# Block two's activations moved by 64 bytes in the on-chip memory

## The reference, cut to what matters

```python
h  = concat([meta_tokens, x])                 # 16 + 256 tokens
hn = rms_norm(h, norm_mix_g)
u, gb_in, gc_in, v_in, ga_lin, gbr_lin = split(hn @ w_in)
y_a = (pooled(u) @ pool_w per group) * pool_scale     # trailing means over 2, 4, 8, 16 tokens
y_b = (gb_in * conv3(gc_in * v_in)) @ conv_out_w
g_a, g_b = split(sigmoid([ga_lin, gbr_lin] + b_gate))
h   = h + (g_a * y_a + g_b * y_b) @ w_o
hn  = rms_norm(h, norm_ffn_g)
gate, up = split(hn @ w_gate_up)              # 2048 -> 2 x 5632
h   = h + (silu(gate) * up) @ w_down          # 5632 -> 2048
out = rms_norm(h, norm_final_g)[16:]
```

## Time and profile before

| what | us |
|---|---|
| median of 3 runs | 3395.7 |
| the runs | 3390.18, 3395.7, 3415.17 |
| the profiled execution, its own time | 3380.61 |
| its span, first to last instruction | 3379.3 |
| first matmul of block two's projections, from the span's start | 1893.8 |
| last of them | 3366.2 |

### The profile page before, as it was taken

One profiled execution on the slowest core, in us unless ns is written; L12 is line 12 of the kernel. 1 busy time (PEld: TensorE's weight loads), 2 busy tenths in 40 slices (PEclk: granted clock), 3 DMA queues, 4 the chain that ended last, 5 costly groups with the idle time before them and its releaser, 6 DMA issues.

```text
span 3379.3 us, 52152 instructions
## 1 busy us (share of the span) xinstructions
PE 3246.4 (96%) x21958; PEld 2812.4 (83%) x21958; DVE 1654.1 (49%) x2688; ACT 1360.2 (40%) x2179; POOL 173.4 (5%) x252
## 2 busy tenths in 40 slices
PE   6899999987999999999799999999999999999998
PEld 2588888873448879888559999999999999999998
DVE  1322233374663254444575675555555655555444
ACT  2322233343443244434354444344444444444443
POOL 3001000001001100100201000000000000000000
PEclk9899999998999999999899999999999999999999
DMA  8633222226654245433434455555555455555554
GB/s 306 252 117 125 94 94 94 86 75 237 237 199 144 99 173 196 161 119 111 146 116 169 158 181 186 183 188 191 196 193 188 169 194 194 195 194 194 195 195 157
DMA packets 152826, 566.09 MB, mean 168 GB/s; under 512 B 17520, under 2 KB 17648, under 8 KB 151440
## 3 DMA queue, kind: packets, MB, share of 16 engines
q1 hardware_dynamic: 146160, 529.52, 45.0%
q0 software_dynamic: 6432, 33.23, 2.7%
HBM read 550.10 MB, written 12.58 MB: 167 GB/s over the span
## 4 chain that ended last, share of the span: by engine, by line
PE 89%; DMA 4%; DVE 3%; ACT 1%; issue 1%; POOL 1%; SPq 0%; DVEq 0%; POOLq 0%; ACTq 0%
PE ps L752 20%; PE ps L754 19%; PE ps L753 19%; PE ps L741 7%; PE ps L743 7%; PE ps L742 7%; DMA sb_raw<-in_stream 4%; PE ps L662 2%; PE ps L874 1%; PE ps L860 1%; PE ps L837 1%; PE ps L853 1%; PE ps L828 1%; PE ps L669 1%; DVE sb_wlo L1296 1%
## 5 line engine op out<-in xcount | busy, mean ns | idle before, releaser
L1296 DVE TENSOR_TENSOR sb_wlo<-sb_raw,sb_whi 128x1024 fp32r<-128x1024 f32 (+1 forms) x814 | 992.6, 1220 | 1316.7 <-ACT sb_whi L946 1315.6
L946 ACT ACTIVATE sb_whi<-sb_raw 128x1024 fp32r<-128x1024 f32 (+1 forms) x818 | 860.0, 1052 | 1091.0 <-PE ps L754 849.0
L752 PE MATMUL ps<-sb_hn_hi,sb_whi 128*128 128x256 f32 (+4 forms) x2944 | 821.8, 279 | 4.7 <-DVE sb_hn_lo L1368 4.1
L754 PE MATMUL ps<-sb_hn_hi,sb_wlo 128*128 128x256 f32 (+4 forms) x2944 | 820.6, 279 | 0.0
L753 PE MATMUL ps<-sb_hn_lo,sb_whi 128*128 128x256 f32 (+4 forms) x2944 | 820.5, 279 | 0.0
L752 PEld LDWEIGHTS ps<-sb_hn_hi,sb_whi 128*128 128x128 f32 x2944 | 555.4, 189 | 5.6 <-DVE sb_hn_lo L1368 4.5
L754 PEld LDWEIGHTS ps<-sb_hn_hi,sb_wlo 128*128 128x128 f32 x2944 | 555.8, 189 | 0.0
L753 PEld LDWEIGHTS ps<-sb_hn_lo,sb_whi 128*128 128x128 f32 x2944 | 555.6, 189 | 0.0
L743 PE MATMUL ps<-sb_whi,sb_lo 128*128 128x512 f32 (+1 forms) x968 | 374.0, 386 | 0.0
L741 PE MATMUL ps<-sb_whi,sb_hi 128*128 128x512 f32 x896 | 353.6, 395 | 0.0
L742 PE MATMUL ps<-sb_wlo,sb_hi 128*128 128x512 f32 x896 | 348.7, 389 | 0.0
(11 more groups left out here) (265 smaller groups left out, 4050.3 us busy)
## 6 DMA issues: line engine op xcount, KB each, us to landing
sb_raw<-in_stream SPq DMA_DIRECT2D x992, 512.0 KB, 3.8
sb_raw<-in_stream SPq DMA_DIRECT2D x18, 384.0 KB, 3.0
sb_T<-in_x POOLq DMA_DIRECT2D x1, 4096.0 KB, 17.3
z_scratch<-sb_scr POOLq DMA_DIRECT2D x16, 256.0 KB, 2.5
sb_zb<-z_scratch POOLq DMA_DIRECT2D x16, 256.0 KB, 3.1
sb_bias<-in_bias POOLq DMA_DIRECT2D x4, 1024.0 KB, 10.1
x_scratch<-sb_T POOLq DMA_DIRECT2D x1, 4096.0 KB, 15.1
sb_T<-in_x POOLq DMA_DIRECT2D x2, 1536.0 KB, 7.5
```

Of the source, the lines that this page charges most:

```text
L752: PE.matmul(o, whi[:, s, w], xh, start=k == 0, stop=False)
L754: mm = PE.matmul(o, wlo[:, s, w], xh, start=False, stop=k == g.kt - 1)
L946: AC.activation(whi[:, s, 0:width], raw[:, r, 0:width], ACT.Copy).then_inc(*hi.up((g.id, c)))
L1296: VE.tensor_tensor(wlo[:, s, 0:width], raw[:, r, 0:width], whi[:, s, 0:width].bitcast(F32), ALU.subtract).then_inc(*lo.up((g.id, c)))
```

## The change

One constant of the layout changes, from 0 to 192.

```diff
-WEIGHTS_AT, ONE_AT, TWO_AT = 64, 64, 0
+WEIGHTS_AT, ONE_AT, TWO_AT = 64, 64, 192
```

## The result

The changed kernel takes 3440.4 us (median of 4 runs, 3435.3 to 3447.2) against 3392.9 us for the kernel before (median of 4, 3387.0 to 3415.2). The ratio is 1.0137, with a 95% interval of 1.0095 to 1.0180.

A forecast was written before the change was run, and what follows sets the result against it. PE's matmul intervals were taken to bound block two; 65.6 + 5.7 + 0.5 = +71.8 us on the 3395.7 us median gave 3467 us, range 3445 to 3494, chance 0.86.

The forecast's parts named there:

- What bounds the kernel: In block two PE is busy almost throughout, so time is the number of matmuls times their start-to-start interval.
- Step (a): Block two's 256-column matmuls at full clock: intervals rise from 113.3 or 117.7 ns to 120.0, together +65.6 us.
- Step (b): Block two's 258-column matmuls, distance 184 to 120: between no change and +11.3 us, middle taken, +5.7 us.
- Step (c): Block two's matmuls of 260, 264 and 272 columns: small shifts if distance counts, none by own start; middle +0.5 us.
- Step (d): Everything else, VectorE, ScalarE, weights' stream and output: nothing in the sum, some 0.1 us at the output's end.
- two readings: Matmul price goes by distance from the weights, or by the moving operand's own start; both give 32 cycles for 256 columns.
- my test for it: Block two's 272-column group after the change: 24.3 us if own start counts, 23.0 if distance does.
- No change: Rival: only equal residues collide, so 128 is as good as 192; time stays 3395.7 us; chance 0.06.
- Faster: Rival: price falls with distance to none at 128; -72.4 us, 3323 us; chance 0.04.
- twice as dear: Rival: 256-column matmuls pay another 16 cycles, 126.7 ns; +134.6 us, 3530 us; chance 0.04.
- The rule of the two independent read ports: Opposing rule: loading the next weights takes nothing from the running matmul, so addresses don't matter and the sum is 0.

The follow-up runs named there:

- the exchange of residues: Two runs against the kernel before: weights at 128, block two at 0, 3446.9 us; weights at 0, block two at 192, 3416.1 us; block one at 64 in both.
- the low parts apart: Kernel before with only the low parts of the weights moved by 64, to 128 modulo 256: 3451.4 us, ratio 1.0172.
- the placement at 64: Kernel before with block two moved to 128 modulo 256, distance 64 from the weights, block one unchanged: 3429.4 us, ratio 1.0128.
- the other residues with the same distance: Against the kernel before, weights at 0, block one at 64, block two at 192, keeping distance 192: 3416.1 us, ratio 1.0058.

## Why the prediction was right or wrong

**What bounds the kernel: right.** PE waits 4.1 us on its longest wait in both, VectorE and ScalarE are as busy as before, and the 51.0 us that block two gained are all intervals.

**Step (a), 256 columns: the mechanism right, the size wrong. This is the step that failed.** Forecast 120.0 ns and +65.6 us. Measured 118.7 ns, and +50.1 us by the sum of the intervals over the 10,366 of these matmuls that another of block two follows (1182.9 to 1233.0 us). The price at distance 128 was taken from 272 columns at that distance and from 256 columns at distance 0, both 32 cycles. For 256 columns at 128 it is 12.0 ns, 28.8 cycles. A row with the right residues but another number of columns gave the sign, not the third digit; and 1.3 ns times ten thousand is 14 us, which by itself is the way out of the range. The range had no term for it: its ends came from steps (b) and (c) and from the spread of the runs of before, while the term with all the matmuls stood without bounds of its own. The 28 to 32 cycles of the other rows in the same list would have given them. (A slip beside it moves nothing: a third slow stretch, of some 46 matmuls at 2023 us, was left out, worth 0.2 us.)

**Step (b), 258 columns: the lower end.** +5.7 us taken, ends 0 and +11.3. Measured: 210.6 us before and 210.2 after, -0.3 us. **Step (c):** +0.5 us taken; measured +0.3 (260), +1.0 (264) and 0.0 (272), so +1.3.

The measured terms add up to the 51.0 us of the stretch. On the median of before that would have been 3444 us, and 3440.4 was measured. The remaining 3.5 us are inside the interval of the ratio, which on this kernel reaches from 32 to 61 us.

**Step (d): right**, in that nothing else shows in the sum (ScalarE's idle time in the stretch is 829 us, a little more than the 800 given). The output's four transfers took 2.8 us each before and 2.9 after. Their queue's share of the 16 engines over the last 14 us, before and then after:

```profile
q1 hardware_dynamic: 576, 2.10, 36.6%
```

```profile
q1 hardware_dynamic: 576, 2.10, 37.7%
```

The effect is small but real: the mean of the output's 512 packets of 4096 bytes is 158.9 ns in each of the six profiles with block two at 0, and 163.7 to 163.8 in the four with it at 192, 3% more. By the Trainium skill, DMA: Bandwidth & Descriptors, How a descriptor splits into AXI transactions, it would be about 5%, an estimate from the page's beats; the traces agree in the direction and show less.

**The cause: one of two readings, and my test for it pointed at the wrong one.** I wrote that the 272-column group would tell them apart, 24.3 us for the own start and 23.0 for the distance. It took 24.3. But the exchange of residues shows that the distance decides for 256 columns: 118.7 ns at distance 128 whether the operand begins at 192 or at 0, 113.3 at distance 192 from either. The matmuls of block one with exchanged roles say the same for 512. Why a distance is dear, and what in the chip collides, no run shows. What failed in the test was its premise that a distance of 64 is as cheap as 192 for any number of columns.

**The rivals.** *No change* is refuted with its mechanism, since 128 is not as good as 192. *Faster* and *twice as dear* are refuted by the same row, 118.7 ns. The rule of the two independent read ports (the Trainium skill, TensorE: Matmul & The Clock Gate, What happens when you issue a matmul) doesn't describe these streams: moving only pieces that are loaded, one in three, cost block two 4.4 to 4.9 ns per matmul. The page's back-to-back gap, 109.2 ns for 256 columns, leaves the loads out by its own words, and no stretch reached it. At the lower clock the traces don't speak against the rule: 213.3 ns for 256 columns at distances 0, 64, 128, 192 and 224.

**Profile against median.** The first profile of before, 3380.6 us, was one of its best executions, and I carried the difference to the median as if it were noise. It has a structure: at distance 192 a stretch may run at 113.3 or 117.8 ns, and the timed runs of that kernel spread over up to 43 us (13 runs), while with block two at distance 128, 64 or 0 and with the low parts apart the spread is 4 to 14 (4 runs each). That the executions near 3420 us are those whose FFN stretch fell into the 117.8 ns rhythm is likely by its price (6,315 matmuls x 4.4 ns = 28 us) and by the time of the placement at 64. It isn't shown: all three profiles of that kernel, and three at the other residues with the same distance, have the long stretch fast; between the three of that kernel the part ahead of block two differs by 9.5 us and block two by only 4.5; and in one comparison seven runs of it stayed within 5 us. What picks the rhythm is open too.

No placement tried beats the kernel before. Its residues, distance 0 for the block with mostly 512-column matmuls and 192 for the one with 256, are the cheapest found for each.

## What to carry to other kernels

Where each matmul comes with a load of its own, look at the time from start to start per operand pair and compare it with the columns over the clock; two groups of one shape with different intervals point to addresses. Then change the residue of one operand at a time, since a change of one residue moves start and distance together, and try the real number of columns, because the best distance for 512 was the worst for 256. And give the term that holds most of the instructions its own error: a nanosecond on it is worth more than a whole unknown on a small one.

## What the runs showed of the hardware

- With float32r operands and a 128x128 load beside each matmul, the interval between matmuls depends on where the moving operand and the stationary pieces begin relative to each other: 113.3 to 120.0 ns for 256 columns, 226.7 to 233.3 for 512, at 2.4 GHz. At 1.2 GHz there was no price at any distance that the traces hold (213.3 ns for 256 columns at 0, 64, 128, 192 and 224).
- The price is not per pair: with one load in three at another distance, all three intervals rose, to 117.8 and 118.2 ns on average.
- A stretch keeps its interval, whatever VectorE and ScalarE do beside it. The changed kernel repeats 120, 119, 115, 117, 122 ns for hundreds of microseconds: from 2700 to 3100 us any five in a row take 593 or 594 ns, while VectorE is busy 199 us and ScalarE 171.
- One program at the same addresses can run a stretch in either of two such rhythms (113.3 or 117.8 ns at distances 192 and 64), and an execution mixes them.
- A 4096-byte packet of the output took 158.9 ns from a source at 0 modulo 256 and 163.8 ns from one at 192.
